# A hybrid layer with 32 experts: gate/up weights in 4 MB transfers, reading order made by the writers, a first pair without scatter

## The reference

```python
h = rmsnorm(x, g_ffn)                       # 256 x 1024
logits = h @ w_router + b_router; top 4 of 32; gates = softmax(top values)
for e in range(32):
    gu = h @ w_gu[e] + b_gu[e]              # w_gu[e]: 1024 x 2048, 8 MB
    gate = minimum(gu[:, :1024], 7); lin = clip(gu[:, 1024:], -7, 7)
    act = gate * sigmoid(1.702 * gate) * (lin + 1)
    y = act @ w_down[e] + b_down[e]         # w_down[e]: 1024 x 1024, 4 MB
    out += combine[:, e] * y
return rmsnorm(x + out, g_final)
```

## Time and profile before

| | us |
|---|---|
| median of 3 runs | 1038.88 |
| lowest and highest | 1036.74, 1042.88 |
| profiled execution | 1037.48 |
| its span, first to last instruction | 1034.8 |

### The profile page before, as it was taken

How to read it: one execution, slowest core, us unless ns; L and a number is a source line. 1 busy time by engine, 2 the same in 40 slices (tenths; PEclk the granted TensorE clock), 3 DMA queues, 4 the chain that set the end, 5 groups by cost and what they waited for, 6 DMA issues and landing times.

```text
span 1034.8 us, 12029 instructions
## 1 busy us (share of the span) xinstructions
PE 956.8 (92%) x4841; PEld 427.4 (41%) x4841; DVE 284.8 (28%) x537; ACT 133.7 (13%) x200; POOL 18.2 (2%) x20
## 2 busy tenths in 40 slices
PE   7999999999999989989899999989898999989895
PEld 7988443434343333434243243434343343424331
DVE  6954331222221213122121213113121312213113
ACT  7634001010100000000000000000000000000102
POOL 0500000000000000000000000000000000000000
PEclk9999999999999999999999999999999999999999
DMA  9569899999999999999999999999999999999993
GB/s 359 205 261 396 343 380 415 428 428 430 429 426 429 429 429 428 430 429 426 429 429 429 428 430 429 426 429 429 428 428 430 429 426 429 429 428 428 428 427 146
DMA packets 34489, 419.41 MB, mean 405 GB/s; under 512 B 5300, under 2 KB 5960, under 8 KB 9864
## 3 DMA queue, kind: packets, MB, share of 16 engines
q1 hardware_dynamic: 34432, 419.16, 96.1%
q10 hardware_dynamic: 40, 0.01, 0.0%
HBM read 418.10 MB, written 1.05 MB: 405 GB/s over the span
## 4 chain that ended last, share of the span: by engine, by line
PE 53%; DMA 41%; DVE 4%; issue 1%; ACT 0%; SPq 0%; ACTq 0%; DVEq 0%
PE ps L909 50%; DMA raw<-in_w_down 37%; DMA raw<-in_w_gu 3%; PE ps L1142 2%; DVE woutl L653 1%; DVE xT L750 1%; DMA win<-in_w_in 1%; PE ps L1193 0%; ACT sm L477 0%; PE ps L998 0%; DVE mxs L670 0%; DVE sm L665 0%; PE ps L1166 0%; DVE outs L900 0%; PE ps L1052 0%
## 5 line engine op out<-in xcount | busy, mean ns | idle before, releaser
L909 PE MATMUL ps<-raw,xT 128*64 128x512 f32 x2048 | 459.6, 597 | 23.1 <-DMA raw<-in_w_gu 22.8
L909 PEld LDWEIGHTS ps<-raw,xT 128*64 128x64 f32 x2048 | 140.9, 137 | 322.0 <-issue 265.1
L909 PE MATMUL ps<-raw,actT 128*64 128x512 f32 x1024 | 233.4, 597 | 24.6 <-DMA raw<-in_w_down 24.6
L909 PEld LDWEIGHTS ps<-raw,actT 128*64 128x64 f32 x1024 | 72.2, 136 | 161.2 <-issue 147.4
L840 DVE TENSOR_TENSOR biased<-ps,biasT 128x1024 f32<-128x1024 f32 x32 | 39.2, 1224 | 335.5 <-PE ps L1142 335.5
L541 ACT ACTIVATE gu<-ps 128x1024 f32<-128x1024 f32 x32 | 32.8, 1024 | 527.8 <-PE ps L909 527.8
L857 DVE TENSOR_TENSOR acc<-ps,acc 128x512 f32<-128x512 f32 x64 | 41.2, 686 | 135.4 <-PE ps L909 135.4
L750 DVE TENSOR_TENSOR xT<-ps,gT 128x512 f32<-128x512 f32 x32 | 22.1, 691 | 180.1 <-PE ps L909 180.1
L909 PE MATMUL ps<-ysc,dispT 64*128 64x512 f32 x272 | 67.8, 615 | 0.8 <-DVE ysc L891 0.8
L909 PEld LDWEIGHTS ps<-disp,h 128*128 128x128 f32 x512 | 61.6, 196 | 12.4 <-issue 12.2
L909 PE MATMUL ps<-disp,h 128*128 128x128 f32 x512 | 64.8, 285 | 0.2 <-DVE disp L744 0.2
(11 more groups left out here) (163 smaller groups left out, 428.6 us busy)
## 6 DMA issues: line engine op xcount, KB each, us to landing
raw<-in_w_gu SPq DMA_DIRECT2D x128, 2048.0 KB, 32.6
raw<-in_w_down SPq DMA_DIRECT2D x64, 2048.0 KB, 34.7
win<-in_w_in SPq DMA_DIRECT2D x16, 512.0 KB, 12.5
wout<-in_w_out SPq DMA_DIRECT2D x4, 1024.0 KB, 9.4
acc<-in_x SPq DMA_DIRECT2D x2, 512.0 KB, 3.8
out<-outs SPq DMA_DIRECT2D x2, 512.0 KB, 3.1
gfin<-in_g_final SPq DMA_DIRECT2D x1, 512.0 KB, 9.5
cst<-in_consts SPq DMA_DIRECT2D x1, 402.0 KB, 7.7
```

Of the source, the lines that this page charges most:

```text
L909: return pe.matmul(out_, lhsT, rhs, start=start, stop=stop, skip_group_check=shared)
```

## The change

- Gate/up goes in transfers of 4 MB, two buffers at once, four rows of w_gu (32 KB) per partition. Such a transfer waits until both buffers are free, and PE waits for it once, ahead of its first half. Only the gate/up of the second pair's first expert comes in four pieces of 2 MB. Down stays in 2 MB: four of the eight rows that a partition now has.
- h2 is written by ACT in the order in which PE reads it, and so is gu (L511, L541): the steps are now on the read side of ACT, and PE reads in a row.
- The first iteration is written out, without its scatter. The down biases and the combine weights have tiles of their own (`bdown`, `combT`), and the last iteration's `scatter` adds them by one more product for each half. The zeroing of ysc and dispT on POOL goes, and the cast at L733.
- The first chunk of w_in goes ahead of x, and the constants go one chunk later. ACT and DVE split that chunk ahead of the first tokens.

```diff
+        bdown = at("bdown", [P, 512], F32, 132 * KB)
+        combT = at("combT", [P, TT, P], F32, 134 * KB)
 ...
-            for t in range(TT):
-                sp.dma_start(acc[:, t, :], x[0, t * P:(t + 1) * P, :]).then_inc(x_loaded[t], 16)
             for h in range(2):
                 for c in range(DC):
                     sp.dma_start(win[:, h, c, :], ...)
-                    if h == 0 and c == 1:
+                    if h == 0 and c == 0:
+                        for t in range(TT):
+                            sp.dma_start(acc[:, t, :], x[0, t * P:(t + 1) * P, :]).then_inc(x_loaded[t], 16)
+                    if h == 0 and c == 2:
 ...
+            def load_gu(e, u, s, half):
+                dst = raw[:, PLACE[s]:PLACE[s] + 2].rearrange("p b r n -> p (b r n)")
+                src = w_gu[0, bass.ds(e, 1), 4 * u * P:4 * (u + 1) * P, :].rearrange("a (p r) n -> p (a r n)", r=4)
+                sp.dma_start(dst, src).then_inc(gu_loaded[half][u], 16)
+            def load_down(e, u, s, half):
+                src = w_down[0, bass.ds(e, 1), :, :].rearrange("a (p r) n -> p (a r) n", r=8)
+                sp.dma_start(raw[:, PLACE[s]].rearrange("p b (r n) -> p (b r) n", r=2),
+                             src[:, 4 * u:4 * u + 4, :]).then_inc(down_loaded[half][u], 16)
 ...
             sp.wait_ge(win_used, 1)
-            for c in range(GU_U):
-                load(0, c, c)
+            for u in range(2):
+                load_gu(0, u, 2 * u, 0)
             sp.wait_ge(ypool_done, 1)
-            load(1, 0, 4)
             sp.wait_ge(probs_turned, 6)
-            load(1, 1, 5)
+            load_gu(1, 0, 4, 1)
             sp.wait_ge(half_projected, 1)
-            load(1, 2, 6)
             sp.wait_ge(projected, 3)
-            load(1, 3, 7)
+            load_gu(1, 1, 6, 1)
 ...
+            def free(i, k):
+                sp.wait_ge(unit_used, i * ITER_U + (PRE_U + k - RAW + 1))
+            # in an iteration:
+                if first:
+                    for k in range(GU_U):
+                        free(i, at_ + k)
+                        load_gu_piece(nxt, k, buffer(half, at_ + k))
+                elif not last:
+                    for u in range(2):
+                        free(i, at_ + 2 * u + 1)
+                        load_gu(nxt, u, buffer(half, at_ + 2 * u), 0)
 ...
-                act.activation(h2[:, t, :], acc[:, t, :], ACT.Copy, scale=rs[:, t:t + 1]).then_inc(scaled, 1)
+                act.activation(h2[:, t, :].rearrange("p (u r q) -> p u r q", u=2, r=4),
+                               acc[:, t, :].rearrange("p (u q r) -> p u r q", u=2, r=4), ACT.Copy,
+                               scale=rs[:, t:t + 1]).then_inc(scaled, 1)
 ...
-                act.activation(gu[:], ps[:, GU[half]:GU[half] + 2, :].rearrange("p a b -> p (a b)"),
-                               ACT.Copy).then_inc(gu_copied, 1)
+                act.activation(gu[:].rearrange("p (r q) -> p r q", r=8),
+                               ps[:, GU[half]:GU[half] + 2, :].rearrange("p a b -> p (a b)").rearrange(
+                                   "p (q r) -> p r q", r=8), ACT.Copy).then_inc(gu_copied, 1)
 ...
-            def gu_unit(half, c, s, value):
+            def gu_unit(half, c, s, count, pieces=False):
                 r = c % 2
-                if r == 0:
-                    pe.wait_ge(raw_loaded[s], value)
+                if pieces and r == 0:
+                    pe.wait_ge(gu_piece_loaded[c // 2], 16)
+                elif not pieces and c % 4 == 0:
+                    pe.wait_ge(gu_loaded[half][c // 4], count * 16)
 ...
-            def scatter(t):
+            def scatter(t, last):
                 for h in range(2):
-                    rows = slice(h * SLOTS, (h + 1) * SLOTS)
+                    rows, biases = slice(h * SLOTS, (h + 1) * SLOTS), slice(h * SLOTS, h * SLOTS + E)
+                    if last:
+                        mm(ps[:, M[h], :], combT[biases, t, :], bdown[biases, :], stop=False)
                     for a in range(2):
-                        ins = mm(ps[:, M[h], :], dispT[rows, a, t, :], ysc[rows, a, :], start=a == 0, stop=a == 1)
+                        ins = mm(ps[:, M[h], :], dispT[rows, a, t, :], ysc[rows, a, :],
+                                 start=a == 0 and not last, stop=a == 1)
```

More of the change, by code:

```diff
@@ L342, in _, with iteration @@
             sp.dma_start(gfin[:], g_final.rearrange("(a n) -> a n", a=1).broadcast_to([P, D])).then_inc(gfin_loaded, 16)
+            for h in range(2):
+                sp.dma_start(bdown[h * SLOTS:h * SLOTS + E, :], b_down[0, :, h * 512:(h + 1) * 512]).then_inc(bdown_loaded, 16)
             sp.wait_ge(rounds_ready, 1)
             last_two = sp.snap(sp.value_load(further[0:1, 0:1], min_val=0, max_val=T // SLOTS - 1) * (PAIRS // 2) + (PAIRS // 2 - 1))
-            def iteration(j, half, last):
+            def free(i, k):
+                sp.wait_ge(unit_used, i * ITER_U + (PRE_U + k - RAW + 1))
+            def iteration(j, half, last, first=False):
                 i = j * 2 + half
@@ L349, in iteration @@
                 nxt = pair_of(i + 1) * 2
[L350 to L358, removed]
-                        load(nxt, k - GU_U - DN_U, s)
-                    elif k < ITER_U:
-                        load(a + 1, k - GU_U - DN_U, s)
-                    else:
-                        load(nxt + 1, k - ITER_U, s)
-            with sp.Fori(0, last_two) as j:
+                for u in range(DN_U):
+                    free(i, GU_U + u)
+                    load_down(a, u, buffer(half, GU_U + u), 0)
+                at_ = GU_U + DN_U
+                if first:
[6 more added lines that the diff above has]
+                        load_gu(nxt, u, buffer(half, at_ + 2 * u), 0)
+                if not last:
+                    at_ += GU_U
+                for u in range(DN_U):
+                    free(i, at_ + u)
+                    load_down(a + 1, u, buffer(half, at_ + u), 1)
+                if not last:
+                    for u in range(2):
+                        free(i, ITER_U + 2 * u + 1)
+                        load_gu(nxt + 1, u, buffer(half, ITER_U + 2 * u), 1)
+            iteration(0, 0, False, first=True)
+            iteration(0, 1, False)
+            with sp.Fori(1, last_two) as j:
                 iteration(j, 0, False)
@@ L884, in iteration @@
                     clip(i * 2 + 2, e)
-            with dve.Fori(0, last_pair) as i:
+            iteration(0, False)
+            with dve.Fori(1, last_pair) as i:
                 iteration(i, False)
@@ L1197, in iteration @@
                 pe.wait_ge(act_ready, i * 2 + 1)
[L1198 removed]
+                down_unit(0, 0, buffer(half, 4), i + 1)
                 if not last:
@@ L1202, in iteration @@
                     gather(0)
-                    pe.wait_ge(added, i * 4 + TT + 4)
+                    if not first:
+                        pe.wait_ge(added, i * 4 - 4 + (TT + 4))
                     gather(1)
@@ L1234, in last_scatter @@
                             ins.then_inc(scattered, 1)
-            with pe.Fori(0, last_two) as j:
+            iteration(0, 0, False, first=True)
+            iteration(0, 1, False)
+            with pe.Fori(1, last_two) as j:
                 iteration(j, 0, False)
```

126 lines of the change are left out of this document (55 added, 71 removed).

## The result

| | before | after |
|---|---|---|
| median, us (9 runs each) | 1039.68 | 1048.81 |
| lowest and highest | 1036.74, 1042.88 | 1045.63, 1054.12 |
| profiled execution | 1037.48 | 1054.12 |
| its span | 1034.8 | 1052.3 |
| PE busy in the span | 956.8 | 975.3 |

The kernel is slower, by about 1%: after over before is 1.0095, 95% interval 1.0073 to 1.0117 (by the two medians alone it is 1.0088). The forecast was no change (1038.9), with a range up to 1044.5.

The account below looks back on a forecast made before the run. From the 381st microsecond the chain of waits runs from one landing of weights to the next, so the weight stream and PE's work after it set the time. -0.4 +0.2 -4.4 +4.6 = 0.0 us gave 1038.9, range 1033 to 1044.5.

Parts of the forecast that it names:

- Rate, -4.4: Gate/up stream: 32 KB rows save 9.6 ns per row, 77 ns per 4 MB transfer, over 57 transfers: -4.4 us.
- Rival (a): Gate/up stream: rate doesn't change, as rows are cut in two or the loss belongs to bytes; 1043.3, chance 0.2.
- (b): Rival: gate/up gains -8.8 for -4.4, or PE running through covers the end; 1034.5 by either, 1030 both; chance 0.2.
- (c): Rival: 32 KB steps between partitions slow every weight transfer; 1052.7 at 1% less rate, far bound 1088; chance 0.1.
- Start, -0.4: Kernel start, x behind w_in's first chunk: PE begins between 9.9 and 11.3, -1.1 to +0.3 us, middle -0.4.
- Loads ahead of the first pair: Expert 1's gate/up as two 4 MB loads: first down transfer at most 1 us late, nobody waits on it.
- First pair without scatter, +0.2: Iteration 0: PE saves 4.6 us, given back as units 16 and 17 wait for unit 9; 3 us gap, +0.2.
- Copies, 0: ACT's copies of gu and h2 into reading order: covered by a down block and by routing, taken at nothing.
- End, +4.6: Last iteration: PE starts gate/up after 4 MB, biases add 1.9; end 1026.8 against 1022.2, +4.6 us, bounds +2.7 to +5.5.
- the 38.1: Last iteration: 38.1 us from PE's last wait on gate/up to the last down product, with no later wait.

Follow-up runs that it names:

- x_first: The changed kernel with x ahead of w_in again, the rest of the change kept; 1046.21 us, ratio to before 1.0039 to 1.0080.
- best_first: best with the first iteration's fourth gate/up load also in 2 MB transfers, each issued as its own buffer comes free; 1034.28 us.
- best: The changed kernel with x ahead of w_in, very last gate/up in 2 MB pieces, 64-row bias products, these in the 15th iteration; 1034.44 us.
- bias64: The changed kernel with bias products of 64 rows instead of 32, the added rows zeroed by POOL; 1043.90 us.
- no_bias: The changed kernel without the four products that add the down biases in the last iteration; 1038.98 us.
- last_pieces: The changed kernel with the very last expert's gate/up in four 2 MB transfers, each with its own wait; 1042.75 us.

## Why the prediction was wrong, step by step

- **Rate, -4.4: right**, in size (58.45 us a pair for 58.4), in its price per row (9.5 ns for 9.6) and in its cause. Rival (a), no gain, and the part of (b) with more than the row price fall with it. So does (c): with steps of 32 KB the stream is faster, 431 GB/s at 300 to 900 for 429. The other part of (b), an end covered by PE, did not come either.
- **Start, -0.4: wrong**, +1.6 at uT in the mean of the profiled executions, and 2.6 by x_first's median. The step "PE begins between 9.9 and 11.3" took 7.1 to 8.5 for x's landing and 2.6 us for PE's work from the earlier trace rows. x landed at up to 9.35, and the turns alone took 3.3 to 3.65 instead of 1.97: a duration was carried over from rows where PE had been busy ahead of it to a place where it had been idle.
- **Loads ahead of the first pair: right in kind.** Unit 8 went out at 111.31, 2.5 later than before; 1 had been allowed, the rest is the late start.
- **First pair without scatter, +0.2: right in kind.** The gap stands where it was put, and best_first shows that it is the wait for unit 9. Its size was put at 3 us; it is (428-239) x 5/428 = 2.2 in x_first, 2.1 in best, up to 2.9 (180 GB/s) in bias64, where the clock had made unit 9 late, and 0.5 in after (387). Each turn of gu became 0.14 us shorter (1.09 for 1.23), not 0.27.
- **Copies, 0: right.** gu's copy is 1025 ns for 1024, though its reads are at steps of 8; h2's became 2.14 us, beside routing. The weight load of gu's turn is 141 ns.
- **End, +4.6: the step that failed**, in two of its terms. "The biases moved here, 4 records in each scatter, 2x0.96 = 1.9" took 0.24 us a record from rows of 64-row products that overlap; the records have 32 rows, cost 0.53, and cost the others their overlap: 8.0 us. And every duration behind the last wait was taken at full clock. The wait for gate/up there before was 1.24 us long, with 16 records in 3.65 us behind it; the new one was forecast at about 4 us, and that it might cost more than itself was not asked. It did: +1.75 to +2.8 on the next 16 records. The sum of the profiled execution: gate/up landed at 986.1 for 983.7, and 53.6 us for 38.1 came after it; of these 15.5, 6.1 are the bias records at full clock over the 1.9, and 9.4 are the clock, after the wait and after the biases. x_first has the same products and no second fall; its first and last row of this stretch:

```profile
985.15 5.35 PE L919 MATMUL ps<-raw,xT 128*64 128x512 f32 x16 [2.98 <-DMA raw<-in_w_gu]
...
1027.54 3.65 PE L919 MATMUL ps<-raw,actT 128*64 128x512 f32 x16
```

  That is 1031.19 - 985.15 = 46.04 us, the 38.1 with 6.1 for the biases and 1.75 for the clock behind the wait. Of the 2.4 us by which after's gate/up landed late, 0.9 are the start and the first gap (see above), and 0.9 the last pair, whose landing came 59.4 us behind the one before (986.09 - 926.70) for 58.45 in the earlier ones. The last pairs of x_first, no_bias and bias64 took 59.3 to 60.0 as well; why is not shown.
- **By the medians**: 1048.8 - 1038.9 = 9.9 us too low. Of these 0.8 are before's own median, 1039.68 over nine runs where 1038.88 had been taken; the change made 9.1. The biases' term is 9.8 instead of 1.9, +7.9, and the start +1.6 instead of -0.4, +2.0. That the two come to 9.9 as well is partly luck: the clock behind the last wait is in neither, the scatter of each median is 1 us or more, and the parts aren't independent, since the late last gate/up is worth 4.9 by forecast and 6.1 by last_pieces.

The bounds were too narrow for the same reason: "+2.7 (were the bias products free) to +5.5" had no upper case for them, since their shape, 32 rows, was not in any row of the trace and was priced by its nearest neighbour as if it were it.

## What to carry to other kernels

A larger transfer saves a fixed price per row, and pays for it where the stream ends: the consumer starts one transfer later, waits longer, and what comes behind a longer wait can run at half the clock. Take large transfers in the middle, small ones with their own waits for the last load, and move extra work out of the last iteration into one where the engine waits anyway. Products that ran side by side on the two halves of the rows lost that here to extra products of 32 rows, and kept it when these were padded to 64: try the padded shape before leaving a product small. And price an operation whose shape stands in no row of the trace by a range, not by its nearest neighbour.

## What the hardware showed that was not expected

- 32-row float32 products among 64-row ones: 12 records in 5.92 us (0.49 each, none overlapping); padded to 64 rows, 3.73 us; eight 64-row records alone, 1.92 us.
- Over the profiled executions of all the changed kernels, PE's waits for gate/up of 2.09 to 2.26 us left the clock up (16 records in 3.65 us). Behind waits of 2.43 to 2.72 us it was sometimes low and sometimes not, and behind every one of 2.73 to 4.47 us it was low (5.0 to 6.7 us for 16 records). It also fell without a wait, behind the 32-row products in four of the seven kernels that had them, and in iteration 0 at the first gather, where PE had waited for only 0.6 us.
- ACT read PSUM at steps of 32 bytes at full pace (gu's copy of 128x1024 float32, 1025 ns for 1024), while its read of SBUF at steps of 16 bytes took nearly twice the time (h2's copy, 2.14 us for 1.15).
- A row of 32 KB went as one packet, and each row cost an engine 9.5 ns beyond its bytes.
